# Gates multiplied on ScalarE instead of GpSimd in a PEER stage, and one table set for logarithm and exponential

## The reference, cut to what matters

```python
def rms_norm(x, g):
    xf = x.astype(jnp.float32)
    y = xf * lax.rsqrt(jnp.mean(xf * xf, axis=-1, keepdims=True) + EPS)
...
def peer_ffn(h, wq, subkeys, u_tab, v_tab):
    ...
    e1 = jnp.take_along_axis(i1, pos // PEER_TOPK, axis=-1)
    e2 = jnp.take_along_axis(i2, pos % PEER_TOPK, axis=-1)
    idx = e1 * PEER_NKEYS + e2
    gate = jax.nn.softmax(best, axis=-1).astype(h.dtype)
    ...
        act = jax.nn.gelu(jnp.einsum('phkd,pd->phk', u_tab[ib], tb)) * gb
        return jnp.einsum('phk,phkd->pd', act, v_tab[ib])
```

## Time and profile before

| | |
|---|---|
| median of the three runs | 3577.81 us |
| the profiled execution | 3578.59 us |
| its span | 3576.7 us |
| PE busy | 3462.9 us, 97% |
| DVE busy | 2373.3 us, 66% |
| ACT busy | 1548.0 us, 43% |
| POOL busy | 941.5 us, 26% |

### The profile page before, as it was taken

The page is one execution under the profiler, slowest core; times in us unless marked ns, Lnnn a source line. Parts: engine busy times, 40 slices in busy tenths (PEclk is TensorE's granted clock), DMA queues, the critical chain, the costliest instruction groups (busy, mean ns, idle before and its releaser), DMA issues.

```text
span 3576.7 us, 55854 instructions
## 1 busy us (share of the span) xinstructions
PE 3462.9 (97%) x22489; PEld 3167.0 (89%) x22489; DVE 2373.3 (66%) x3955; ACT 1548.0 (43%) x2424; POOL 941.5 (26%) x705
## 2 busy tenths in 40 slices
PE   8999999999899999999999999999999999999998
PEld 8988999999797778788767887899999998999998
DVE  7435465545744646555477553549998997898997
ACT  7254443222635444322358353334336664333333
POOL 4010023111401002311111400115544565344441
PEclk9999999999999999999999999999999999999999
DMA  4211232222121123322222022336766998999995
GB/s 151 67 52 60 77 124 83 94 90 89 65 77 55 64 77 124 100 94 95 100 71 77 31 95 71 106 104 232 241 215 226 326 328 297 354 364 365 368 367 198
DMA packets 191825, 552.34 MB, mean 154 GB/s; under 512 B 20176, under 2 KB 69456, under 8 KB 191184
## 3 DMA queue, kind: packets, MB, share of 16 engines
q1 hardware_dynamic: 130080, 376.51, 30.6%
q0 software_dynamic: 36864, 134.23, 10.8%
q10 hardware_dynamic: 24624, 38.01, 2.9%
HBM read 504.64 MB, written 44.04 MB: 153 GB/s over the span
## 4 chain that ended last, share of the span: by engine, by line
PE 75%; DVE 16%; ACT 3%; DMA 3%; issue 1%; POOL 1%; ACTq 0%; DVEq 0%; POOLq 0%
PE PSM L316 16%; PE PSM L317 16%; PE PSM L318 16%; PE PSM L210 5%; PE PSM L3173 5%; PE PSM L3174 5%; PE PSM L3175 5%; DVE PARTS L283 3%; DMA CH<-peer_rows_dram,MQ 2%; DVE MQ L3404 2%; DVE CH L3421 2%; DVE MQ L3400 1%; ACT PARTS L274 1%; PE PSM L1060 1%; DVE MH L1740 1%
## 5 line engine op out<-in xcount | busy, mean ns | idle before, releaser
L274 ACT ACTIVATE PARTS<-RAW 128x1024 fp32r<-128x1024 f32 x612 | 645.6, 1057 | 898.5 <-PE PSM L318 482.9
L316 PE MATMUL PSM<-UX,PARTS 128*128 128x264 f32 (+3 forms) x2912 | 974.5, 335 | 28.7 <-DVE UX L2296 4.9
L317 PE MATMUL PSM<-UX,PARTS 128*128 128x264 f32 (+3 forms) x2912 | 957.6, 329 | 0.0
L318 PE MATMUL PSM<-UX,PARTS 128*128 128x264 f32 (+3 forms) x2912 | 957.1, 329 | 0.0
L283 DVE TENSOR_TENSOR PARTS<-RAW,PARTS 128x1024 fp32r<-128x1024 f32 (+1 forms) x612 | 746.5, 1225 | 305.6 <-ACT PARTS L274 305.4
L316 PEld LDWEIGHTS PSM<-UX,PARTS 128*128 128x128 f32 x2912 | 550.6, 189 | 80.0 <-issue 12.3
L317 PEld LDWEIGHTS PSM<-UX,PARTS 128*128 128x128 f32 x2912 | 551.0, 189 | 29.6 <-issue 1.7
L318 PEld LDWEIGHTS PSM<-UX,PARTS 128*128 128x128 f32 x2912 | 549.7, 189 | 29.8
L3173 PE MATMUL PSM<-AC,PARTS 128*128 128x384 f32 x1024 | 343.6, 336 | 5.4 <-DVE AC L3469 5.4
L3174 PE MATMUL PSM<-AC,PARTS 128*128 128x384 f32 x1024 | 342.7, 335 | 0.0
L3175 PE MATMUL PSM<-AC,PARTS 128*128 128x384 f32 x1024 | 342.7, 335 | 0.0
(11 more groups left out here) (506 smaller groups left out, 6032.5 us busy)
## 6 DMA issues: line engine op xcount, KB each, us to landing
RAW<-w_ff_dram SPq DMA_DIRECT2D x128, 512.0 KB, 3.2
RAW<-peer_u_dram SPq DMA_DIRECT2D x128, 512.0 KB, 4.5
RAW<-peer_v_dram SPq DMA_DIRECT2D x128, 512.0 KB, 6.3
RAW<-w_in_dram SPq DMA_DIRECT2D x116, 512.0 KB, 3.3
acts_dram<-MQ ACTq DMA_DIRECT2D x128, 192.0 KB, 4.0
MQ<-acts_dram SPq DMA_DIRECT2D x128, 192.0 KB, 6.3
RAW<-w_mix_o_dram SPq DMA_DIRECT2D x32, 512.0 KB, 3.3
MQ<-gates_dram SPq DMA_DIRECT2D x32, 512.0 KB, 7.9
```

What stands on the lines that cost most here:

```text
L274: e.activation(p[:, 0:1024], self.raw.of(i), ACT.Copy).then_inc(S.sem, S.tick("w", i))
L316: e.matmul(dst, wh[k], xh_[k][:, lo:hi], start=(k == 0), stop=False, skip_group_check=True)
L317: e.matmul(dst, wh[k], xl_[k][:, lo:hi], start=False, stop=False, skip_group_check=True)
L318: m = e.matmul(dst, wl[k], xh_[k][:, lo:hi], start=False, stop=(k == kk - 1), skip_group_check=True)
```

## The change

There are two edits. First, GpSimd no longer multiplies in steps 74 to 121; its part of the block is now only gathers (and the low halves of tiles before step 74, as before). The gate goes into ScalarE's one-hot instead: relu(gate - gate x distance), with minus the gate as the scale and the gate as the bias, which differ from token to token, so that the one instruction of 128 x 512 becomes four of 128 x 128. Minus the gate is kept in `Gn`, the unused last 128 columns of three Y buffers, and is made by one more eviction (128 x 128) at three places far ahead of its use. The matrix engine no longer waits for GpSimd in `gates`. Second, seven preloads (in `rstd_act`, `roots_act`, `root`, `onorm_act` and three places of the mixer's program) name a table set with both the logarithm and the exponential instead of the function Ln.

```diff
@@ rstd_act, and in the same way roots_act, root, onorm_act and three places of the mixer's program
         def rstd_act(e, tag, n, rs, scale, *done):
-            e.preload_act_table(ACT.Ln)
+            e.preload_act_table_set("natural_log_exp_and_others")
             e.wait_ge(T.sem, T.at(done[0], tag, *done[1:]))
@@ the PEER block
         Y = [qb(oY + i * 512, 512) for i in range(4)]
+        Gn = [x[:, TD:T2] for x in Y[0:3]]
@@ peer_pe, gates
                     if half:
                         e.wait_ge(S.sem, S.at("onA", i4))
-                        e.wait_ge(G.sem, G.at("onB", i4))
                     else:
                         e.wait_ge(V.sem, V.at("onA", i4))
@@ peer_act, one_hots
                 e.wait_ge(S.sem, S.at("off", i4))
-                e.activation(a, a, ACT.Relu, bias=con["ones"][:, 0:1], scale=-1.0).then_inc(S.sem, S.tick("onA", i4))
+                g, u0 = Gn[FILLS[n][0]], t0 - 128 * FILLS[n][0]
+                for i in range(4):
+                    e.activation(a[:, 128 * i:128 * i + 128], a[:, 128 * i:128 * i + 128], ACT.Relu, bias=Gt[:, t0 + i:t0 + i + 1],
+                                 scale=g[:, u0 + i:u0 + i + 1]).then_inc(S.sem, S.tick("onA", i4))
@@ peer_act
                 for n in turn_at(i):
                     e.wait_ge(T.sem, T.at("e12", n))
+                    e.activation(Gn[n], PSM[:, ps.of("e12", n), 256:384], ACT.Copy, scale=-1.0).then_inc(S.sem, S.tick("minus", n))
@@ peer_pool
-            def one_hots(n, t8):
-                i4 = four_at(n, t8) + 1
-                t0 = FILLS[n][1] + 8 * t8 + 4
-                o = onB[i4 % 4].rearrange("p (t n) -> p t n", t=4)
-                e.wait_ge(V.sem, V.at("onB", i4 - 1))
-                e.tensor_tensor(o, o, Gt[:, t0:t0 + 4].unsqueeze(2).to_broadcast([128, 4, 128]), MUL).then_inc(
-                    G.sem, G.tick("onB", i4))
...
-                for n, t8 in gates_at(i + 1):
-                    one_hots(n, t8)
```

## The result

| | before | after |
|---|---|---|
| median of the runs made side by side | 3576.84 us (3575.73 to 3579.18) | 3534.26 us (3531.97 to 3534.96) |
| ratio, 95% interval | | 0.9879, 0.9862 to 0.9896 |
| profiled execution, its span | 3578.59, 3576.7 us | 3533.88, 3532.1 us |
| PE busy, PE waiting | 3462.9, 113.7 us | 3448.0, 84.1 us |

The change gains 42.6 us, 1.2%.

A forecast was written before the change was run, and what follows sets the result against it. PE, at 97% of the span, was taken as the bound, so gains had to come from its waits: 15 (norms) + 13 (passes) + 2 (stage end) = 30 us, giving 3547.8 us, range 3540 to 3562.

The forecast's parts named there:

- Edit 2, the norms: Table loads between logarithm and exponential, 14 places on the chain: 15 us gained, between 9 and 17.9.
- Step (b), the hold: VectorE's four one-hots, line 3404, freed of GpSimd's multiplication: 1.83 to 1.11 us, 1.48 if a gather's issue holds them.
- the plain loop: VectorE's own work over three gate steps: 19.3 us before, forecast 15.6, or 16.4 with two groups held.
- Step (c), the passes: Gate stage: PE at 5.95 us a step throughout, 13 of 14.2 us gained, 8 as the lower end.
- The loop through the gather: Gather, dot products and one-hots over three gate steps: 19.45 us falls to 18.0, 6.00 a step, if gathers take 7.6.
- Step (e), the end of the stage: PE's 4.12 us wait before the second half of the block: between 0 and 4.1 us gained, 2 taken.
- Step (d), ScalarE: Gate stage: one relu becomes four, 0.73 to 1.65 us; ScalarE keeps 0.76 us of waiting a step, so no cost.
- The hold on the gathers: Rival, 0.13: gather issues hold line 3404 instead, the gate stage gains at most 3 us; 3560.
- The norms that hide: Rival, 0.12: other ScalarE and VectorE work is as late as the exponential, norms give only 5 us; 3558.
- the doubled row: Rival, 0.03: each saved table switch frees twice its row, 30 us for the norms; 3533.
- ScalarE as the bound: Rival, 0.04: above 0.60 us per relu ScalarE's gate step exceeds PE's 5.95; at 0.9 the kernel slows to 3602.
- Little out of both: Rival, 0.05: 0 to 7 us gained, as transfers take back in the second half what the first wins.

The follow-up runs named there:

- fewer: Changed kernel without the preload in rstd_act at seven norms where the set is still active; 3530.19 us, ratio to before 0.987.
- fewest loads: Changed kernel without those seven rstd_act preloads and three more, two of root and one of onorm_act; 3531.29 us.
- tables only: Kernel before with the seven preloads changed and nothing else; 3560.79 us, ratio 0.9962.
- ScalarE + 4: Changed kernel with four more distances, overwritten by the real ones, in each of ScalarE's one-hot groups; 3555.37 us.
- one-hots first: Kernel before with VectorE's four one-hots (line 3404) moved ahead of the large one (line 3400), GpSimd still multiplying; 3568.25 us, ratio 0.998.
- Late VectorE: Changed kernel with five extra reductions on VectorE, 1.1 us each, in step 120 alone; 3542.41 us.
- times one: Changed kernel with GpSimd multiplying by one at the old place and PE waiting for it again; 3559.81 us, ratio 0.9962.

## Why the prediction was wrong, and what of it was right

**Edit 2, the norms: 15, right.** Up to the first pass of gates the four executions with the old preloads took 2689.6 to 2695.9 us, mean 2691.9; the ten with the new ones (fewer and fewest loads aside) 2675.3 to 2681.5, mean 2677.6. That is 14.3, and the last exponential adds 1.3. The measured 14.5 of tables only agrees within its interval. The eight loads of line 865 are worth nothing, as forecast. A load costs its row of 1.28 us. The drain that the Trainium skill names ("ScalarE: Activation LUTs", "What ACT_TABLE_LOAD costs") would, as an estimate from its 2.66 us, have made the edit worth twice this; the trace has 1.28 us between logarithm and exponential with the load and 0.02 without, so it does not show.

**Step (b), the hold: right in kind, with the smaller price.** Groups take 1.11 us, those inside a gather's issue too, so the plain loop became 15.6 and not 16.4.

**Step (c), the passes: right in kind, 13 forecast, some 16 measured.** The passes take 296.5 to 297.6 us with the hold and 280.3 to 281.9 without it, means 297.0 and 280.8 (the two runs with VectorE's own work, ScalarE + 4 and the one-hots first aside). In the first profile 14.2 of it lie behind the pass at 2716.58, just as forecast; the other 2 are the first interval, 8.42 us before and 6.40 to 7.75 after, part of it at 1.2 GHz. Gathers did not slow down: 7.5 us in the median, 7.6 before. The loop through the gather, at 18.0 us against PE's 17.85, was overpriced: with two more one-hots my formula gives 18.0 + 2 x 0.63 = 19.3 us, 6.4 a step, and passes were 5.95 nearly throughout. The 6.42 us a step of before fit the other loop, VectorE's plain work of 19.3 us in three steps, 6.43 each; from 2800 to 2950 us VectorE waits for gathered rows 4.1 us in all.

**Step (e), the end of the stage: the step that failed.** It read "between 0 and 4.1 us. I take 2, because the transfers are close behind it". It was worth 8: 4.1 from the last pass to the second half, and 3.9 behind it in the first tiles, a part I had left out of the bound (551.2 without the norm's 1.3, the mean of four kernels with the hold, against 547.3). Of the 3.9, waits for late tiles are 1.5 in the mean (0.5 to 3.5), and 2.3 are PE's first products at 1.2 GHz behind the long wait. The reason that I gave for 2 failed as well: VectorE still waits for its rows there as long as before (10.4 and 10.2 us), and the wait of PE fell by 3.2 all the same; the same stretch moved 340 instead of 311 GB/s. Late VectorE shows that VectorE's lead at that point decides. I bounded the term by one wait row, where later tiles ran late too and the clock fell behind the wait.

**The first pass, counted at nothing**, gave some 0.6 us of wait for the hold itself (2.23 and 2.56 in tables only and times one, 1.85 after). The rest of the first profile's 4.23 was that execution's own.

**The clock, not counted.** Between the two profiles PE did 9 us less of lost work at 1.2 GHz (61.0 against 43.0 busy, half of the difference). This is no further term: the stretches lie inside the terms above. In the first tiles it belongs to the change (2.3 us, step (e)). Ahead of the first pass the two profiles differ by 6.5 us of lost work, but over all executions the means are alike, so that there it looks like chance; two executions of one kernel differ by 5.7 us in all. Not all of the gain is in rows of waiting, either: of the 44.6 us of span 29.6 are PE's waits and 15 its busy time. What is left of the 15 beside the 9 of the clock lies mostly in the passes, where the ends of products are modelled (16 us longer passes in times one have 12.7 us of recorded waits).

The terms as measured are 15.6 + 16 + 8 + 0.6 = 40 us, against 42.6 between the medians. The remaining 2 to 3 us lie inside the interval of the ratio and are not explained. Against the 30 forecast, 6 are missing at step (e), 3 at step (c) and 1 at the norms and the first pass.

**Step (d), ScalarE: right** to a hundredth (1.65 forecast, 1.66; 0.76 and 0.73), and the two runs with extra work put its edge where the step had it.

**The rivals.** The hold on the gathers is refuted by the ten groups inside a gather's issue. The norms that hide and the doubled row are refuted by the 14.5. ScalarE as the bound needed over 0.7 us a step more. Little out of both is refuted by the 42.6 and by the transfers, which carry 361 GB/s at the start of the second half. None of the cases let VectorE's lead, and with it PE's clock, carry past the stage, which is the one that came.

## What to carry to other kernels

When an engine that was the bound of a stage is relieved, look past the stage's end: the lead that it builds is spent in the next stage, and the term is bounded by all the waits there and by what the granted clock costs behind them, not by the one longest wait. A hold of one engine by another moved here to whichever instruction came second, so that reordering gave back 7 us and removing the instruction 25. Before an experiment that puts a cost back, add up the cost over the whole period of the loop, its long cases too.

## What the runs showed of the hardware

A 128 x 512 multiplication on GpSimd (1.05 us) stretched VectorE's four one-hots from 1.11 to 1.83 us. When the multiplication came second it was the one that stretched, to 1.95 us, and the VectorE instruction behind it stretched too. A gather's issue left the one-hots inside it at 1.11 us and was itself longer: 1.98 us with one-hots inside, 1.68 beside line 283, 0.94 with at most a dot product beside it. PE's waiting time repeats within 1 us from one execution to the next (113.7 and 114.2; 84.1 and 84.9), while its busy time at 1.2 GHz in the same kernel was 61.0 and 49.5 us. In one place the low clock did come with the wait: at the start of the second half it fell in all eight executions with a wait of 2.8 to 4.7 us there, and in none of the eight with less.
